# Two-layer trunk on one core: queries of the first layer left unnormalised, small inverses in PSUM, operations and fill products moved

## What is computed

```python
# layer 0
qkv = silu(causal_depthwise_conv(u @ w_in))
q = l2norm(q) * 128 ** -0.5 ; k = l2norm(k)          # per token and head; l2norm(x) = x * rsqrt(sum(x*x) + EPS)
tri = eye + strict_lower(kb @ k.T * decay)            # per chunk
sol = triangular_solve(tri, [v*beta, k*beta*exp(g)])
attn_intra = q @ k.T * decay ; q_g = q * exp(g)
o_i = q_g @ S + attn_intra @ v_new ; S = S * g_last + k_tail.T @ v_new
o = rmsnorm(o, o_norm) * silu(z)                      # o * rsqrt(mean(o*o) + EPS)
h = x + o @ w_out
# layer 1: stick-breaking attention over all earlier keys, times silu(gate), @ w_out
# output : rmsnorm(h)
```

## Time and profile before

| | us |
|---|---|
| runs of the kernel | 1349.78, 1349.96 (median), 1350.57 |
| the profiled execution's own time | 1350.38 |
| its span (first to last instruction) | 1348.6 |
| granted TensorE clock, mean | 0.995 |

### The profile page before, as it was taken

How to read it: one execution, slowest core, us unless ns; L and a number is a source line. 1 busy time by engine, 2 the same in 40 slices (tenths; PEclk the granted TensorE clock), 3 DMA queues, 4 the chain that set the end, 5 groups by cost and what they waited for, 6 DMA issues and landing times.

```text
span 1348.6 us, 18350 instructions
## 1 busy us (share of the span) xinstructions
PE 1285.0 (95%) x6829; PEld 1064.7 (79%) x6829; DVE 984.7 (73%) x1701; ACT 699.8 (52%) x1112; POOL 577.7 (43%) x380
## 2 busy tenths in 40 slices
PE   7997999999999999999997999999999999998997
PEld 5786888888787878878885778788787878786786
DVE  5587888979898889886339767787778777777413
ACT  6355446364637364453226556656566656665303
POOL 6533333333333333432125694646565464632300
PEclk9998999999999999999999999999999999999999
DMA  7210110211111021206215111222111111118503
GB/s 194 76 46 16 32 48 16 63 33 47 48 42 53 16 63 32 60 31 221 82 32 187 32 32 33 57 60 71 48 47 48 47 47 48 54 56 293 175 1 125
DMA packets 106858, 91.42 MB, mean 68 GB/s; under 512 B 3106, under 2 KB 92307, under 8 KB 106771
## 3 DMA queue, kind: packets, MB, share of 16 engines
q1 hardware_dynamic: 106770, 90.25, 22.1%
HBM read 66.65 MB, written 23.59 MB: 67 GB/s over the span
## 4 chain that ended last, share of the span: by engine, by line
PE 70%; DVE 13%; ACT 7%; issue 7%; POOL 2%; DMA 0%; DVEq 0%; SPq 0%; ACTq 0%
PE psum L526 21%; PE psum L681 17%; PE psum L695 5%; PE psum L2540 4%; PE psum L2514 3%; PE psum L2527 2%; DVE stick L2101 2%; DVE terms L1938 2%; PE psum L2425 2%; PE psum L543 2%; PE psum L654 2%; PE psum L2336 1%; DVE small_L L1923 1%; PE psum L2409 1%; PE psum L2446 1%
## 5 line engine op out<-in xcount | busy, mean ns | idle before, releaser
L526 PE MATMUL psum<-u_hi,w_hi 128*128 128x512 f32 x640 | 260.4, 407 | 4.1 <-DVE u_lo L1651 1.7
L526 PE MATMUL psum<-u_hi,w_lo 128*128 128x512 f32 x640 | 258.9, 404 | 0.0
L526 PE MATMUL psum<-u_lo,w_hi 128*128 128x512 f32 x640 | 257.8, 403 | 0.0
L493 POOL TENSOR_TENSOR w_lo<-w_raw,w_hi 128x1024 fp32r<-128x1024 f32 (+1 forms) x45 | 107.9, 2398 | 237.3 <-ACT w_hi L488 225.4
L526 PEld LDWEIGHTS psum<-u_hi,w_hi 128*128 128x128 f32 x640 | 120.9, 189 | 29.8 <-issue 4.3
L526 PEld LDWEIGHTS psum<-u_hi,w_lo 128*128 128x128 f32 x640 | 120.9, 189 | 24.1 <-issue 1.9
L526 PEld LDWEIGHTS psum<-u_lo,w_hi 128*128 128x128 f32 x640 | 121.1, 189 | 20.8 <-issue 0.5
L1793 DVE SCALAR_TENSOR_TENSOR late<-raw,cols,late 128x1024 f32<-128x1024 f32 x72 | 128.2, 1781 | 1.8
L623 POOL TENSOR_TENSOR w_lo<-w_raw_b,w_hi 128x512 fp32r<-128x512 f32 x40 | 58.4, 1462 | 113.0 <-ACT w_hi L607 113.0
L488 ACT ACTIVATE w_hi<-w_raw 128x1024 fp32r<-128x1024 f32 (+1 forms) x45 | 45.9, 1020 | 109.5 <-PE psum L526 109.3
L2101 DVE TENSOR_TENSOR_SCAN stick<-soft 128x1024 f32<-128x1024 f32 (+3 forms) x64 | 101.2, 1582 | 0.2
(11 more groups left out here) (312 smaller groups left out, 3297.2 us busy)
## 6 DMA issues: line engine op xcount, KB each, us to landing
w_raw<-in_a_w_in SPq DMA_DIRECT2D x33, 512.0 KB, 4.1
w_raw<-in_b_w_in SPq DMA_DIRECT2D x16, 512.0 KB, 5.3
w_raw_b<-in_b_w_in SPq DMA_DIRECT2D x16, 512.0 KB, 5.4
b_rows<-o_part SPq DMA_DIRECT2D x14, 512.0 KB, 3.8
o_rows<-o_part_a SPq DMA_DIRECT2D x12, 512.0 KB, 3.6
x_stage<-in_x SPq DMA_DIRECT2D x8, 512.0 KB, 7.4
out<-fin_o SPq DMA_DIRECT2D x8, 512.0 KB, 2.6
u_lo<-b_rows SPq DMA_DIRECT2D x7, 512.0 KB, 8.4
```

Source lines behind the costliest of these rows:

```text
L493: G.tensor_tensor(lo_tiles(key), raw_tiles(key), hi_tiles(key).bitcast(F32), ALU.subtract).then_inc(lo_done, 1)
L526: mm = PE.matmul(psum[:, half], (w_hi, w_hi, w_lo)[part][:, buffer(key), k], (u_hi, u_lo, u_hi)[part][:, k, half * HALF:(half + 1) * HALF] ...
```

## The change

**Queries.** q is no longer squared for a sum, nor split, summed, or scaled. `qT` is `conv` times `eg` at s = 5 in one operation, and the grams at s = 4 take `conv` itself. In place of the scale ACT squares q by halves (`square_q`, with the factor 128·sqrt(EPS), 128x512 from SBUF) at s = 5 (second half) and s = 13 (first half, ahead of `inv_first`), and DVE adds it to `o_sq` (`add_q`) at s = 12 and s = 0.

**Operations moved.** The copy of an output half out of PSUM goes from DVE to ACT, right behind `o_sq`. The sum of the second half's squares goes on PE from s = 0 to the end of s = 1, its Ln and Exp on ACT to s = 2; for the last head it goes from before the last groups to behind the second of them. `o_part_a` of the first half goes on DVE from s = 17 to s = 18, behind `rhs`. The masks of level 1 go on POOL from s = 6 to s = 11. An activation table is loaded at s = 22 instead of with the squares.

**Small inverses.** `small_T` lies in PSUM (bank 6), `row_L` has its own SBUF tile.

**Layer 2.** The last two steps of `STEP_FILL` go from (0, 2), (15, 23) to (0, 8), (12, 20): six products more ahead of the scores of step 7, six fewer behind them. DVE takes a finished group of products at the start of step 7, and the next ahead of the exponent. `FIRST_FILL` is 12 for head 0.

```diff
-HI_AT, LO_AT = (16, 4), (17, 13)
+HI_AT, LO_AT = (16, 4), (18, 13)
+MASK_AT = 11
-STEP_FILL = ((12, 23), (10, 15), (9, 13), (8, 11), (0, 15), (0, 12), (0, 2), (15, 23))
-FIRST_FILL = 6
+STEP_FILL = ((12, 23), (10, 15), (9, 13), (8, 11), (0, 15), (0, 12), (0, 8), (12, 20))
+FIRST_FILL = (12,) + (6,) * (H - 1)
...
-        small_T = sd("small_T", [P, NC, SMALL])
+        small_T = psum[:, 6, 0:NC * SMALL].rearrange("p (n c) -> p n c", c=SMALL)
...
+            def square_q(h, half):
+                if half == 0:
+                    if h > 0:
+                        o_added.wait(act, h - 1, 1)
+                elif h > 1:
+                    o_added.wait(act, h - 2, 2)
+                silu_kq.wait(act, h, 2)
+                A.activation(q_sq_first[:, :] if half == 0 else q_sq_second[:, h % 2], conv[:, 0, half_range(half)],
+                             ACT.Square, scale=P * sqrt(EPS)).then_inc(q_sq_done.handle, 1)
...
                 A.activation(o_sq[:, :], psum[:, 3], ACT.Square).then_inc(osq_done.handle, 1)
+                A.activation(o_nrm[:, :], psum[:, 3], ACT.Copy, scale=cols[:, ONORM_COL:ONORM_COL + 1]
+                             ).then_inc(o_copied.handle, 1)
...
+                if s == 5:
+                    square_q(h, 1)
+                if s == 13:
+                    square_q(h, 0)
...
-            def copy_o(t, half):
+            def add_q(t, half):
                 osq_done.wait(dve, t, half + 1)
-                V.tensor_scalar(o_nrm[:, :], psum[:, 3], cols[:, ONORM_COL:ONORM_COL + 1], None, ALU.mult
-                                ).then_inc(o_copied.handle, 1)
+                q_sq_done.wait(dve, t, 2)
+                V.tensor_tensor(o_sq[:, :], o_sq[:, :], q_sq_first[:, :] if half == 0 else q_sq_second[:, t % 2], ALU.add
+                                ).then_inc(o_added.handle, 1)
...
-                V.tensor_tensor(flat(qT[:, c]), flat(qT[:, c]), eg, ALU.mult).then_inc(qg_done.handle, 1)
+                V.tensor_tensor(flat(qT[:, c]), conv[:, 0], eg, ALU.mult).then_inc(qg_done.handle, 1)
...
+                    if s == NC - 1:
+                        fill.to(STEP_AT[2 * s + 1])
                     exponent(*ahead)
...
-                    for n in range(2):
-                        if n == 1 and t >= 1:
-                            sum_squares_o(t - 1, 1)
-                        sq_lo_done.wait(pe, h, n + 1 if h > 0 else 2)
-                        for half in range(2):
-                            for i, part in enumerate((sq_hi[:, n], sq_lo[n][:, :])):
+                    sq_lo_done.wait(pe, h, 1)
+                    for half in range(2):
+                        for i, part in enumerate((sq_hi[:, :], sq_lo_k[:, :])):
...
+                        if bk == 4 and t >= 1:
+                            oln_done.wait(pe, t - 1, 2)
...
                     fill(t, s, done)
-            sum_squares_o(H - 1, 1)
+                    if s == 1 and t >= 1:
+                        if t + 1 < H:
+                            ln_done.wait(pe, t + 1, 1)
+                        sum_squares_o(t - 1, 1)
             for i in range(2 * KB):
                 last_group(i)
+                if i == 1:
+                    sum_squares_o(H - 1, 1)
```

More of the change, by code:

```diff
@@ L17 @@
 from contextlib import ExitStack
-from math import log
+from math import sqrt
 import concourse.bass as bass
@@ L360, in build @@
         o_copied = sig("o_copied", 2)
+        o_added = sig("o_added", 2)
         osum_ready = sig("osum_ready", 2)
@@ L947, in _ @@
             tok_ready.wait(sp, H - 1, 4)
-            norm_done.wait(sp, H - 1, 2)
+            qg_done.wait(sp, H - 1, 1)
+            norm_done.wait(sp, H - 1, 1)
+            q_sq_done.wait(sp, H - 1, 2)
             for k in range(HOME, KB):
@@ L1346, in norm_scale @@
                 osum_ready.wait(act, t, half + 1)
-                A.activation(o_rs[:, :], psum[:, 5 if half == 0 else 2], ACT.Ln, bias=eps_d[:, 0:1], scale=1.0 / P
+                A.activation(o_rs[:, :], psum[:, SUM_BANK], ACT.Ln, bias=eps_o[:, 0:1], scale=1.0 / P
                              ).then_inc(oln_done.handle, 1)
@@ L1358, in square_o @@
                 A.activation(o_sq[:, :], psum[:, 3], ACT.Square).then_inc(osq_done.handle, 1)
+                if half == 1:
+                    og_done.wait(act, t, 1)
+                elif t > 0:
+                    og_done.wait(act, t - 1, 2)
+                A.activation(o_nrm[:, :], psum[:, 3], ACT.Copy, scale=cols[:, ONORM_COL:ONORM_COL + 1]
+                             ).then_inc(o_copied.handle, 1)
             def late_hi(t, half):
@@ L1388, in prepare @@
                 if s == 0:
-                    for n in range(2):
-                        sums_ready.wait(act, h, n + 1)
-                        A.activation(rs_kq[n], banks(4 + 2 * n), ACT.Ln, bias=eps_d[:, 0:1]
-                                     ).then_inc(ln_done.handle, 1)
+                    sums_ready.wait(act, h, 1)
+                    A.activation(rs_k, banks(4), ACT.Ln, bias=eps_d[:, 0:1]).then_inc(ln_done.handle, 1)
                 if s == 1:
-                    for n in range(2):
-                        ln_done.wait(act, h, n + 1)
-                        A.activation(rs_kq[n], rs_kq[n], ACT.Exp, scale=-0.5,
-                                     bias=(0.0, q_scale[:, 0:1])[n]).then_inc(rs_ready.handle, 1)
+                    ln_done.wait(act, h, 1)
+                    A.activation(rs_k, rs_k, ACT.Exp, scale=-0.5).then_inc(rs_ready.handle, 1)
+                if s == 5:
+                    square_q(h, 1)
+                if s == 13:
+                    square_q(h, 0)
                 if s == 2:
@@ L1431, in _ @@
             split_hi(("q", 1))
-            for n in (1, 0):
-                silu_conv(0, 1 - n)
-                square_kq(0, n)
+            for part_no in (0, 1):
+                silu_conv(0, part_no)
+            square_k(0)
+            A.preload_act_table_set(LN_EXP)
             split_hi(("k", 1))
@@ L1437, in _ @@
                 for s in range(SLOTS):
-                    if s == 0 and t >= 1:
+                    if s == 2 and t >= 1:
                         norm_scale(t - 1, 1)
@@ L1890, in recur @@
                 if s == 12:
-                    copy_o(t, 0)
+                    add_q(t, 0)
                 if s == 15:
@@ L1948, in prepare @@
                 if s == 2:
-                    for n, (dst, part_no) in enumerate(((kT, 1), (qT, 0))):
-                        rs_ready.wait(dve, h, n + 1)
-                        V.tensor_tensor(flat(dst[:, c]), conv[:, part_no], rs_kq[n], ALU.mult
-                                        ).then_inc(norm_done.handle, 1)
+                    rs_ready.wait(dve, h, 1)
+                    V.tensor_tensor(flat(kT[:, c]), conv[:, 1], rs_k, ALU.mult).then_inc(norm_done.handle, 1)
                 if s in (4, 5):
@@ L2012, in _ @@
                     if s == 0 and t >= 1:
-                        copy_o(t - 1, 1)
+                        add_q(t - 1, 1)
                     if t + 1 < H:
@@ L2032, in _ @@
                         take(key, half)
-            copy_o(H - 1, 1)
+            add_q(H - 1, 1)
             for i in range(2):
@@ L2334, in sum_squares_o @@
             def sum_squares_o(t, half):
-                osq_done.wait(pe, t, half + 1)
-                PE.matmul(psum[:, 5 if half == 0 else 2], ones[:, :], o_sq[:, :], start=True, stop=True
-                          ).then_inc(osum_ready.handle, 1)
+                o_added.wait(pe, t, half + 1)
+                PE.matmul(psum[:, SUM_BANK], ones[:, :], o_sq[:, :], start=True, stop=True).then_inc(osum_ready.handle, 1)
             def recur(t, s):
@@ L2417, in prepare @@
                 if s == 4:
-                    norm_done.wait(pe, h, 2)
+                    norm_done.wait(pe, h, 1)
+                    silu_kq.wait(pe, h, 2)
                     for half in range(2):
```

117 lines of the change are left out of this document (55 added, 62 removed).

## The result

| | before | after |
|---|---|---|
| median of four runs, us | 1349.87 | 1316.02 (1315.24 to 1316.84) |
| ratio | | 0.9749 (0.9732 to 0.9766) |
| profiled execution's own time, us | 1350.38 | 1316.84 |
| its span, us | 1348.6 | 1314.9 |

What follows compares the result with a forecast made beforehand. PE, busy 95% of the span, was taken as the bound: fewer matmuls or fewer holes win. Layer 1's 26.2 plus layer 2's 12.0 made 38.2 off 1350.38, or 1312.2; forecast 1312 us, range 1304 to 1329.

Steps and rivals of the forecast that it cites:

- q's sums, 7.4 us: Layer 1, PE: four 128x512 matmuls per head, 32 in all at 0.23 us, go; nothing hides them; 7.4 us saved.
- The waits for `o_sq`, `rhs` and `state`, 18.6 us with a price of mark plus 0.27: Layer 1, PE: all three close; 20 waits, 13.2 us of marks plus 20 × 0.27, 18.6 us saved.
- The reason for `state`: Layer 1, DVE: `small_T` in PSUM keeps `terms` from lasting 2.06 us beside `w_lo`; result 0.7 us earlier, against 0.5 needed.
- (a): Layer 1, POOL: with masks gone from s = 6, `w_lo` starts 1.5 us sooner, meets `small_L`'s subtraction; up to 1.05 later.
- (b): Layer 1 substitution, DVE: PSUM costs 0.066 us more in each of 31 operations on `small_T`, 2.0 us per head.
- The slower rival: Layer 1: dependent substitution operations on `small_T` are dear in PSUM; at 0.3 us extra each, 1368 us; chance 0.04.
- Head 0, 2.5 + 1.1 us: Head 0's preparation, PE: 2.5 of the 3.7 us `inv_first` wait goes, between 0 and 3.9; the `sq_lo_q` wait gives 1.1.
- The square of q ahead of `inv_first`, −2.5: Layer 1, ACT at s = 13: new work leaves a hole costing 0.35 us, seven times; between nothing and −6.
- The last sum of layer 1, −0.9: End of layer 1: sum moves 2.7 us later, its chain arrives later at a wait; costs 0.9, between 0 and 2.7.
- Layer 2, 12.0 us: Layer 2, step 7: waits for `stick` and `b_raw` close, 2.0 us per head in six heads; nothing in the seventh.
- DVE comes no earlier: Rival, layer 1: thin margins miss, `state` keeps its hole, half of `rhs` stay, turn waits 1 us more; 1327, chance 0.17.
- Layer 2's holes only move: Rival, layer 2: next attention turn delayed equally, or a hole opens behind step 7; 12.0 us not won, 1324, chance 0.14.

## Why the prediction was right, and where it was off

The direction and the mechanism were right, and the time lies 4 us above the forecast, inside the range. Layer 1 was to give 26.2 us and gave 24.5; with the two falls of the clock taken out (2.4 us that the kernel before lost, 1.6 that the changed one did) the edits gave 23.7. Layer 2 was to give 12.0 and gave 9.2. By the steps of the sum:

- **q's sums, 7.4 us.** Right: 0.94 per head when put back, 7.5 in eight.
- **The waits for `o_sq`, `rhs` and `state`, 18.6 us with a price of mark plus 0.27.** Right. Put back one at a time the last two cost 1.08 for a mark of 0.82 and 0.76 for 0.50; `o_sq` cost 0.75 for 0.45. That is 0.26 to 0.30 over the mark each time.
- **The reason for `state` was half right.** Blocked `terms` was the cause, but PSUM was not the only cure: the moved masks do the same. I had booked the masks as a cost alone, (a). As a cost they were sized well (0.64 us measured, "up to 1.05" said).
- **(b), PSUM dearer by 0.066 us in 31 operations, 2.0 us per head.** This step failed. The same forms of the substitution in both places:

```profile
L1968 DVE TENSOR_REDUCE psum<-terms 128x8 f32<-128x104 f32 x8 | 2.1, 259 | 0.0
...
L1963 DVE TENSOR_TENSOR terms<-row_L_t,psum 128x104 f32<-128x104 f32 x8 | 2.1, 265 | 0.8
```

```profile
L1967 DVE TENSOR_REDUCE small_T<-terms 128x8 f32<-128x104 f32 x8 | 2.0, 252 | 0.0
...
L1962 DVE TENSOR_TENSOR terms<-row_L_t,small_T 128x104 f32<-128x104 f32 x8 | 2.2, 269 | 0.8
```

The reduction takes 7 ns more with its result in PSUM (12 at the most, at 128x120), and the product 4 ns less with one operand there. The 0.066 of the earlier trace rows belong to a copy alone. From `terms` 128x32 to `terms` 128x120 of head 0 it is 7.36 us before (98.06 to 105.42) and 7.38 after (95.18 to 102.56): with the one copy some 0.1 us per head, not 2.0. In the steady heads it cost the forecast nothing, since DVE had more in hand than I said; in head 0's term it stood with its full 2.0. The slower rival fell with it.
- **Head 0, 2.5 + 1.1 us.** Right in its result, partly by chance. The wait for `inv_first` shrank by 3.3 (3.75 to 0.44), more than forecast because (b) was not there, but the next level's turn, which had not waited, now waits 0.52 and loses 0.7: 2.6 in all. The clock that no longer falls behind this wait gave 2.4 more, and nothing in the sum stood for that. The stretch lost 5.35: these 5.0, 0.93 for q's sums of one head, less 0.6 for longer waits behind it and a later start. The 1.1 of `sq_lo_q` lie in the next stretch.
- **The square of q ahead of `inv_first`, −2.5.** Right, 0.34 per head. Missed beside it was a second place of the same kind: the squares of k at slot 21 leave `v_new` where it was while PE arrives earlier: 0.2 per head, six times. I had priced ACT by its idle time in a head, and not by what stands ahead of `v_new`.
- **The last sum of layer 1, −0.9.** Right: from the end of the ordinary products to the hole's end it is 8.81 against 7.99 us. Missed was the last head's first sum: it now waits 0.72 for `add_q`, where it did not wait before, and loses 0.9.
- **Layer 2, 12.0 us.** This is the term that was off: 8.35 in the six heads, and 0.9 in the rest, for which the sum had nothing. The wait for `stick` closed as said. That for `b_raw` lost its mark, but the filler behind it still starts 0.46 us behind its forerunner (885.91, 886.37). The step "while PE has the same products to run" overlooked what comes next: six products fewer follow step 7's scores, PE reaches the second turn of v sooner, and DVE's scan, which has come sooner too, is held up 0.33 us longer by a `w_lo`. So PE waits for `b_v`: 0.25 marked, 0.5 in all, per head. Two products more ahead of that turn close it (58.90 us per head, near the 58.8 forecast). I had only looked for a hole behind step 7, in a rival, and not at the next head's step 0.
- **The clock.** Nothing in the forecast stood for the 1.6 us of the fall at 128.93, nor for the 2.4 us at 110 that went with the long wait.

Of the rivals, "DVE comes no earlier" had its mechanism (`add_q` at 1.18 us beside the masks, by the Trainium skill's rule in "SBUF — State Buffer", section "SBUF: two separate sides"; the trace agrees), but the turn waits for ACT and not for `invT`. The forecast's own sign of being wrong, an `add_q` of more than 1 us, came true without costing a wait. "Layer 2's holes only move" was right for a third of its amount.

Not tried: the copy of the output half on DVE again, DVE's order in layer 2 with the old deal, and another place for POOL's `w_lo` beside the scan. Open is also why the clock falls behind some idle times of 2.3 us and not behind others.

## What to carry to other kernels

A wait on a full engine is worth its mark plus the restart, here 0.26 to 0.30 us, and it closes by moving the one operation that stands ahead of the result, even if the engine's load does not change. When fill is dealt anew, follow it one step further than the hole it closes: what is put ahead of one wait is missing ahead of the next. Gaps of 0.2 us carry no idle mark; compare start-to-start times of like instructions to find them. When a DVE operation is longer than its like elsewhere, look at what POOL does beside it: here its end followed POOL's end, not its own start.
